# Causal attention on one core: the convolution's place on VectorE, an earlier norm of the memory, its filler matmuls spread over more steps, convolution sums in quarters, and four buffers moved

## The reference

```python
u = rmsnorm(h, norm_mix_pre)
bg, cg, xin, q, kc, vc, ksl, vsl, kw, vw, gl = split(u @ w_in)
z = cg * xin
y_conv = bg * conv3(z)                       # causal, 3 taps, one filter a channel, 512 channels
y_att = nsa_mixer(q, kc, vc, ksl, ...)       # three causal branches, 8 heads of 64
mixed = concat(rmsnorm(y_conv, norm_conv_out), rmsnorm(y_att, norm_attn_out))
h = h + rmsnorm(mixed @ w_out, norm_mix_post)
...
mn = rmsnorm(mem, norm_mem)                  # 256 memory tokens
kx, vx = split(mn @ w_kv_x)                  # for the cross attention behind
```

## Time and profile before

| | us |
|---|---|
| median of 3 runs (1782.98 to 1785.0) | 1784.61 |
| the profiled execution, its own time | 1782.14 |
| its span, first to last instruction | 1780.4 |
| PE busy in it | 1681.0 (94%) |
| mean granted TensorE clock | 0.979 |

### The profile page before, as it was taken

One profiled execution on the slowest core, in us unless ns is written; L12 is line 12 of the kernel. 1 busy time (PEld: TensorE's weight loads), 2 busy tenths in 40 slices (PEclk: granted clock), 3 DMA queues, 4 the chain that ended last, 5 costly groups with the idle time before them and its releaser, 6 DMA issues. The chain is left out here.

```text
span 1780.4 us, 22500 instructions
## 1 busy us (share of the span) xinstructions
PE 1681.0 (94%) x8603; PEld 1336.8 (75%) x8603; DVE 643.7 (36%) x1189; ACT 663.6 (37%) x1001; POOL 732.6 (41%) x639
## 2 busy tenths in 40 slices
PE   7989889988989999999989989998999999999999
PEld 5767668767668888878868767666678788888887
DVE  6431665262323111111147364443458341213131
ACT  4223377363344233222245434332554432323230
POOL 5223324363143444454435533332345444545453
PEclk9999899998999999999999999998999999999999
DMA  4243102232131332343222223221145323232321
GB/s 171 74 142 103 60 25 73 71 118 72 48 95 49 122 112 79 96 148 88 85 82 77 95 79 133 83 89 56 48 167 183 95 73 117 82 108 88 102 94 49
DMA packets 155307, 166.06 MB, mean 93 GB/s; under 512 B 14413, under 2 KB 116928, under 8 KB 155200
## 3 DMA queue, kind: packets, MB, share of 16 engines
q1 hardware_dynamic: 144736, 149.11, 26.2%
q10 hardware_dynamic: 10464, 15.51, 2.5%
HBM read 155.69 MB, written 9.30 MB: 93 GB/s over the span
## 5 line engine op out<-in xcount | busy, mean ns | idle before, releaser
L773 POOL TENSOR_TENSOR w_low<-raw,w_high 128x512 fp32r<-128x512 f32 x505 | 670.3, 1359 | 931.7 <-ACT w_high L916 931.3
L916 ACT CAST w_high<-raw 128x2048 fp32r<-128x2048 f32 (+1 forms) x128 | 241.1, 1884 | 251.5 <-PE bank L2306 240.4
L2311 PE MATMUL bank<-xT_high,w_high 128*128 128x512 f32 (+1 forms) x672 | 249.4, 376 | 0.0
L2312 PE MATMUL bank<-xT_low,w_high 128*128 128x512 f32 (+1 forms) x672 | 248.9, 375 | 0.0
L2302 PE MATMUL bank<-w_high,hid_high 128*128 128x512 f32 x432 | 171.9, 398 | 0.3 <-ACT w_high L916 0.3
L2303 PE MATMUL bank<-w_high,hid_low 128*128 128x512 f32 x432 | 169.8, 393 | 0.0
L2223 PE MATMUL bank<-xT_high,w_high 128*128 128x512 f32 (+1 forms) x360 | 154.3, 429 | 5.6 <-DVE xT_low L1527 3.2
L2315 PE MATMUL bank<-xT_high,w_low 128*128 128x512 f32 (+1 forms) x672 | 156.4, 375 | 0.6 <-POOL w_low L773 0.6
L2312 PEld LDWEIGHTS bank<-xT_low,w_high 128*128 128x128 f32 x672 | 127.5, 190 | 22.4
L2225 PE MATMUL bank<-xT_high,w_low 128*128 128x512 f32 (+1 forms) x360 | 144.3, 401 | 0.0
L2311 PEld LDWEIGHTS bank<-xT_high,w_high 128*128 128x128 f32 x672 | 127.4, 190 | 22.4
(11 more groups left out here) (425 smaller groups left out, 2567.2 us busy)
## 6 DMA issues: line engine op xcount, KB each, us to landing
raw<-in_w_in SPq DMA_DIRECT2D x33, 1024.0 KB, 5.0
raw<-in_w_down SPq DMA_DIRECT2D x26, 1024.0 KB, 5.0
raw<-in_w_gate_up SPq DMA_DIRECT2D x44, 512.0 KB, 5.0
raw<-in_w_up SPq DMA_DIRECT2D x16, 1024.0 KB, 5.3
raw<-in_w_kv_x SPq DMA_DIRECT2D x8, 1024.0 KB, 5.4
raw<-in_w_out SPq DMA_DIRECT2D x8, 1024.0 KB, 5.0
gate_dram<-qbuf ACTq DMA_DIRECT2D x20, 256.0 KB, 2.0
sg<-gate_dram ACTq DMA_DIRECT2D x6, 768.0 KB, 5.3
```

What stands on the lines that cost most here:

```text
L773: ins = pool.tensor_tensor(low[:, cs], full[:, cs], high[:, cs], ALU.subtract)
L916: own.tell(act.copy(split_slot(c, wh), split_slot(c, raw)), wh_done)
L2311: pe.matmul(ps[:, t0:t1], ch[:, k, cs], xh[:, k, t0:t1], start=q == 0, stop=False)
L2312: pe.matmul(ps[:, t0:t1], ch[:, k, cs], xl[:, k, t0:t1], start=False, stop=False)
```

## The change

- `conv` and `conv_scaled` run on DVE between the maximum of item s and the copy of item s-1, and no longer behind the copy and `branch_out`.
- The squares of the memory are summed on ACT in step 3 (`STAT_STEP`), DVE scales it in step 4 in place (`mem_nat` and not `stage`), PE transposes it in steps 9 and 10 (`MEM_STEP` 9).
- `kx` pieces begin at step 13: three a step, four in the last.
- The convolution's sums are made of 64 matmuls with 32 columns of weights each, one for each quarter of the partitions, in place of 16 with 128; they and the spread go to bank 3 and not bank 0, which makes PE wait for the second `o_taken` in step 10 and for the scaled tiles in step 14.
- `conv_root` calls a square root on a constant ahead of its wait, and an exponential behind the root.
- Buffers: the diagonal lies over `junk`, the convolution's output has its own place (`y_conv`), and the branch outputs lie in `share2`. That is also `gpost`, so its load waits for all eight `o_taken`, and is issued ahead of the first `vx` load and not ahead of `out`.
- ACT casts the second chunk of `out` ahead of the last square sum of the attention output.

```diff
@@ -39,6 +39,7 @@
...
 HALVES = (slice(0, 64), slice(64, P))
+QUARTERS = tuple(slice(32 * i, 32 * i + 32) for i in range(4))
 ATT_ORDER = (0, 3, 1, 2)
...
@@ -336,8 +337,8 @@
...
         yatt = at("yatt", 53312, [P, ST, S])
-        cdiag = at("conv_scale", 69696, [P, ST, P])
-        branch_early, branch_late = at("branch_early", 73792, [P, 2, S]), at("branch_late", 61504, [P, 2, S])
+        cdiag = nc.alloc_sbuf_tensor_at("conv_scale", [P, ST, P], F32, offset=junk_at)
+        yconv = at("y_conv", 69696, [P, 4, S])
         qn = at("qn", 53312, [P, 2, S])
...
@@ -517,8 +518,8 @@
...
         early, middle, late = pieces("bg"), pieces("cg", "xin"), pieces("kx")
-        CONV_STEP, SUM_STEP, MEM_STEP, KX_STEP = 5, 10, 14, 17
-        KX_N = [4] * 13 + [3] * 4
+        STAT_STEP, CONV_STEP, MEM_STEP, SUM_STEP, KX_STEP = 3, 5, 9, 10, 13
+        KX_N = [3] * 20 + [4]
         assert sum(KX_N) == len(late) and KX_STEP + len(KX_N) == 2 * ST * PER_GROUP + 2
...
@@ -534,7 +535,7 @@
...
-            return (branch_early if ph < 4 else branch_late)[:, ph % 2, :]
+            return share2[:, S * (ph % 2):S * (ph % 2) + S]
...
@@ -623,10 +624,10 @@
...
                 "kx": lambda: (late_mem(), bias_windows()),
-                "out": lambda: post_gain("norm_mix_post", None),
-                "ox": lambda: (post_gain("norm_x_post", ("h", 4)), natural_gain(0, "norm_ffn_pre", pv_done, 2 * ST * PER_GROUP)),
+                "vx": lambda: post_gain("norm_mix_post", o_taken, 2 * ST),
+                "ox": lambda: (post_gain("norm_x_post", h_ready, 4), natural_gain(0, "norm_ffn_pre", pv_done, 2 * ST * PER_GROUP)),
                 "down0": lambda: second_memory(),
-                "gu2": lambda: (post_gain("norm_ffn_post", ("h", 8)),
+                "gu2": lambda: (post_gain("norm_ffn_post", h_ready, 8),
                                 natural_gain(0, "g_mix_2", xn_ready, ntile["hf", 3] + 1)),
...
@@ -657,9 +658,8 @@
...
-            def post_gain(name, after):
-                if after:
-                    sp.wait_ge(h_ready, after[1])
+            def post_gain(name, dead, count):
+                sp.wait_ge(dead, count)
                 sp.dma_start(gpost[:, :], a[name].rearrange("(o d) -> o d", o=1).broadcast_to([P, D]))\
...
@@ -1021,13 +1021,15 @@
...
                 act.wait_ge(conv_y, ct + 1)
-                own.tell(act.activation(stage[:, ct // 2, (ct % 2) * S:(ct % 2) * S + S], bgT[:, ct, :], ACT.Square),
-                         conv_sq)
+                own.tell(act.activation(stage[:, ct // 2, (ct % 2) * S:(ct % 2) * S + S], yconv[:, ct, :],
+                                        ACT.Square), conv_sq)
...
             def conv_root():
+                own.link(act.activation(rms[:, 63:64], eps_col[:, 0:1], ACT.Sqrt))
                 act.wait_ge(conv_ss, 1)
-                own.tell(act.activation(small[:, 40:44], bank[0][:, 0:ST], ACT.Sqrt, bias=eps_col[:, 0:1],
+                own.tell(act.activation(small[:, 40:44], bank[3][:, 0:ST], ACT.Sqrt, bias=eps_col[:, 0:1],
                                         scale=1.0 / 512), conv_rms)
+                own.link(act.activation(rms[:, 63:64], eps_col[:, 0:1], ACT.Exp))
...
@@ -1071,11 +1073,12 @@
...
                     conv_square(s - CONV_STEP - 1)
-                if s == SUM_STEP:
-                    conv_root()
+                if s == STAT_STEP:
                     act.wait_ge(mem_in, 16)
...
                     stat(("mem", 1), mem_nat[:, 1, :], D)
+                if s == SUM_STEP:
+                    conv_root()
                 if SUM_STEP + 2 <= s < SUM_STEP + 4:
...
@@ -1086,6 +1089,7 @@
...
                                             scale=1.0 / 512), rms_done, 3)
+            high(G["out"].chunks[1].n)
             act.wait_ge(o_taken, 2 * ST)
...
@@ -1490,8 +1494,8 @@
...
                     return
-                own.tell(dve.tensor_scalar(stage[:, i % 2, 0:width], SOURCES[phase][:, j, :], rms[:, k:k + 1], None,
-                                           ALU.mult), xn_ready)
+                dst = mem_nat[:, j, :] if phase == "mem" else stage[:, i % 2, 0:width]
+                own.tell(dve.tensor_scalar(dst, SOURCES[phase][:, j, :], rms[:, k:k + 1], None, ALU.mult), xn_ready)
...
@@ -1666,7 +1670,7 @@
...
                 evacuated(dve, G["bg"].tiles[ct])
-                own.tell(dve.tensor_tensor(bgT[:, ct, :], qbuf[:, 0, :], bgT[:, ct, :], ALU.mult), conv_y)
+                own.tell(dve.tensor_tensor(yconv[:, ct, :], qbuf[:, 0, :], bgT[:, ct, :], ALU.mult), conv_y)
...
@@ -1682,8 +1686,8 @@
...
                     g = gcol[:, COL["norm_conv_out"] + ct:COL["norm_conv_out"] + ct + 1]
-                    own.tell(dve.scalar_tensor_tensor(out=qbuf[:, ct % 2, :], in0=bgT[:, ct, :], scalar=g,
-                                                      in1=bank[0][:, :], op0=ALU.mult, op1=ALU.mult), conv_q)
+                    own.tell(dve.scalar_tensor_tensor(out=qbuf[:, ct % 2, :], in0=yconv[:, ct, :], scalar=g,
+                                                      in1=bank[3][:, :], op0=ALU.mult, op1=ALU.mult), conv_q)
...
@@ -1739,6 +1743,10 @@
...
                             s_taken)
+                if CONV_STEP <= s < CONV_STEP + 4:
+                    conv(s - CONV_STEP)
+                if SUM_STEP + 2 <= s < SUM_STEP + 4:
+                    conv_scaled(2 * (s - SUM_STEP - 2))
                 if 1 <= s <= len(ITEMS):
...
@@ -1749,16 +1757,12 @@
...
                     own.tell(branch_out(branch_step(s)), o_taken)
-                if CONV_STEP <= s < CONV_STEP + 4:
-                    conv(s - CONV_STEP)
+                if s == STAT_STEP + 1:
+                    xn("mem", 0, D)
+                    xn("mem", 1, D)
                 if s == SUM_STEP + 1:
                     conv_inverse()
-                    xn("mem", 0, D)
-                    xn("mem", 1, D)
-                if SUM_STEP + 2 <= s < SUM_STEP + 4:
-                    conv_scaled(2 * (s - SUM_STEP - 2))
                 if MEM_STEP + 1 <= s < MEM_STEP + 3:
-                    dve.wait_ge(conv_lo, 4)
                     ql("mem", s - MEM_STEP - 1)
...
@@ -2206,15 +2210,16 @@
...
                     r = NT[i][3] + b
-                    if phase == "mem" and r == NT[ntile["mem", 0]][3]:
-                        pe.wait_ge(conv_q, 4)
+                    if phase == "mem" and j == 0:
+                        evacuated(pe, G["xin"].tiles[2 + b])
                     if r >= 2:
...
                             pe.wait_ge(q_ready, last[6] + r - 2 - last[3] + 1)
-                    src = hna[:, j, :] if phase == "hna" else hsum[:, j, :] if phase == "hm" else \
+                    src = mem_nat[:, j, 512 * b:512 * b + 512] if phase == "mem" else \
+                        hna[:, j, :] if phase == "hna" else hsum[:, j, :] if phase == "hm" else \
                         stage[:, i % 2, 512 * b:512 * b + 512]
...
@@ -2479,6 +2484,8 @@
...
                         pe.wait_ge(o_taken, ph - 1)
+                        if s == SUM_STEP + 4:
+                            pe.wait_ge(conv_q, 4)
                     for g in range(GROUPS):
...
@@ -2489,15 +2496,17 @@
...
                     pe.wait_ge(conv_sq, 4)
+                    pe.wait_ge(o_taken, 2)
                     for j in range(ST):
                         for ct in range(4):
-                            o = (ct % 2) * S + j * P
-                            mm = pe.matmul(bank[0][:, j:j + 1], stage[:, ct // 2, o:o + P], ones[:, 0:1],
-                                           start=ct == 0, stop=ct == 3)
+                            for qs in QUARTERS:
+                                o = (ct % 2) * S + j * P + qs.start
+                                mm = pe.matmul(bank[3][qs, j:j + 1], stage[:, ct // 2, o:o + 32], ones[:, 0:1],
+                                               start=ct == 0, stop=ct == 3)
                     mm.then_inc(conv_ss, 1)
...
                     pe.wait_ge(conv_inv, 1)
-                    pe.matmul(bank[0][:, :], ones[:, :], cdiag[:, :, :], start=True, stop=True).then_inc(conv_bc, 1)
+                    pe.matmul(bank[3][:, :], ones[:, :], cdiag[:, :, :], start=True, stop=True).then_inc(conv_bc, 1)
                 if MEM_STEP <= s < MEM_STEP + 2:
...
```

## The result

The changed kernel takes 1772.88 us (median of 4 runs, 1769.11 to 1773.33), the kernel before in the same comparison 1784.8 (1782.98 to 1785.46). The ratio is 0.9934, with a 95% interval of 0.9921 to 0.9947: about 0.7% faster. The prediction was 1774 us. The profiled execution took 1772.66 us, with a span of 1770.9, against 1782.14 and 1780.4.

A forecast was written before the change was run, and what follows sets the result against it. PE, busy 94% of the span, was taken as the bound, so gains come only where it idles or runs at low clock. Terms summed to -10.7 us, from the median 1784.61 to 1774 us; range 1766 to 1780.

The forecast's parts named there:

- Steps 6 and 7: Filler's waits for the convolution and the low clock behind them go, 6.71 us a step: -3.7 us.
- Steps 8 and 9: No filler; scores wait less for the maximum, the copy comes late next; 9.3 against 10.48 us: -1.2 us.
- steps 3 and 4: Memory's sums of squares on ACT (about 5.8 us) and scalings on DVE (2 us), hidden by filler: cost nil.
- Step 10: Low clock, sums by quarters at 5.7 us, memory transposes added; 13.8 against 9.67 us: +4.1 us.
- Quarters that don't overlap: Rival: each of 128 records costs its lone time, about 222 ns; sums 28 us, time 1797 us; 5 in 100.
- the clock stays up in steps 10 and 11: Rival: without the long waits PE keeps full clock there, some 5 us less; time 1768 us; 18 in 100.
- Step 11: Loses ACT's square sums and DVE's scalings, PE waits 0.3 us for the inverse; 7.0 against 6.59: +0.4 us.
- Steps 12 to 17: Waits and memory transposes go, 11 more filler pieces fit in; 23.8 against 27.52 us: -3.7 us.
- Steps 18 to 33: Twelve steps lose a filler piece, the last gains one, 0.36 us each: -4.0 us.
- `out`: Second chunk cast early; shorter wait, then for `xT_low`, and part of the low clock saved: -2.6 us.

The follow-up runs named there:

- c2: Changed kernel with ACT casting the first `kx` chunk in step 9 and not step 6, so POOL's split no longer meets the third convolution; 1768.98 us, ratio 0.9917.
- b4: Kernel before with only the convolution moved between maximum and copy on DVE; 1773.43 us, ratio 0.9943.
- c4: Kernel before with three edits only: convolution's place, sums by quarters, early cast of the second chunk of `out`; 1771.48 us, ratio 0.9935.
- a2: Changed kernel with the convolution's sums as 32 matmuls of 64 weight columns, alternating between two halves of the partitions; 1772.08 us.
- a3: Changed kernel with the same quarter matmuls, but all 16 of one quarter ahead of the next; 1773.75 us, ratio 0.9948.
- b2: Changed kernel with the old filler, `kx` pieces from step 17, four a step; 1774.06 us, ratio 0.9944.
- b3: Changed kernel without ACT's early cast of the second chunk of `out`; 1773.22 us, ratio 0.9942.
- c1: Changed kernel with ACT casting the memory's high part ahead of the root, and DVE inverting the scale ahead of step 11's maximum; 1770.47 us, ratio 0.9929.
- b1: Changed kernel with the convolution back behind the copy and `branch_out` on DVE; 1771.6 us, ratio 0.9931.
- c3: Changed kernel with both edits, the new order of steps 10 and 11 and the later cast of the first `kx` chunk; 1768.36 us, ratio 0.9909.
- a1: Changed kernel with the convolution's sums again as 16 matmuls of 128 weight columns, still in bank 3; 1772.15 us, ratio 0.994.

## Why the prediction was right, point by point

**Steps 6 and 7: right** in place and size. The two convolutions' waits are gone and each step takes 6.71 us.

**Steps 8 and 9: wrong**, +2.0 for -1.2. The step that failed is "In steps 5 to 7 that cover is some 5.5 us of pieces, enough to hide it." The 7.39 us beside POOL stood in the prediction, but wasn't set against the cover of step 7. That convolution begins 2.8 us into the step, behind the maxima, and at 7.1 us ends at 201.93, while PE is at the next step's transposes from 199.82. So PE waited 2.26 us, the low clock came at 203.78 and not 205, and the memory's transposes met it whole. c2 shows the cause: without POOL's split beside it, step 8 is as forecast. Step 9 stays at 7.45 us there, for 6.5: the low clock accounts for that 1.0.

A second step failed with it, in the passage on steps 3 and 4: DVE's two scalings of the memory delay a maximum "which is wanted a step later. Cost nil". First a scaling in the kernel after, then the start of the third convolution and PE's wait in b4, which has no scalings in step 4:

```profile
178.93 0.75 DVE L1498 TENSOR_SCALAR mem_nat<-mem_nat,rms 128x1024 f32<-128x1024 f32 x1
```

```profile
194.74 0.69 DVE L1662 TENSOR_TENSOR zT<-zT,bank 128x512 f32<-128x512 f32 x1
201.90 0.30 PE L2200 MATMUL bank<-ident,prob 128*128 128x128 f32 x1 [1.02 <-DVE probT L1750]
```

From the scalings on DVE has next to no idle time in the kernel after until step 10. Its third convolution begins 2.80 us into step 7 and takes 7.08, in b4 1.97 into the step and takes 6.68. So PE waits 2.26 us and not 1.02, and step 8 takes 5.02 and not 3.79 (3.79 in c4 too, which leaves the memory where it was). The memory's place was not taken back by itself, so the 1.2 us are read from kernels that differ in more. b4 isn't the forecast come true either: its steps 8 and 9 take 9.40 us, but without the memory's 1.7 the prediction would have had 7.6.

**Step 10: wrong**, -2.0 for +4.1, the largest error. The step that failed is "I take the middle, 5.7 us (45 ns each)". Measured are 1.16 us, 9 ns each, below the lower bound of 3.9, which supposed that a quarter of the columns costs a quarter of the time, one matmul behind the other. The bound is for the low clock, but half of it, 1.9 us as an estimate for the full one, is still more than was measured. It left out that four quarters can work at once. The rival "Quarters that don't overlap" at 222 ns a record falls too, but the forecast's own 45 ns were also a price for one matmul behind the other. The floor of 60 cycles in the Trainium skill (TensorEngine Tiling (Array Packing), Instruction Overhead), 6.4 us here, doesn't hold for matmuls that take turns over the quarters: at full clock 60 cycles are 25 ns, and 9 were measured. It fits a2 and a3 better, with 31 and 33 ns. The same page of the Trainium skill (TensorEngine Tiling (Array Packing), Key Properties) also says that different tiles can load weights and multiply in parallel. a3 against the kernel after shows it, 33 ns against 9. The other 3.0 us are the clock, which was full again from 213.00, ahead of the sums and not behind them; a wait of 1.58 us for the second `o_taken`, where 0.2 were counted, took 1.4 back. 5.7 - 1.16 + 3.0 - 1.4 = 6.1, the whole miss. In part the rival "the clock stays up in steps 10 and 11" came true, though the clock didn't stay up: it fell earlier and rose earlier.

**Step 11: right by two errors.** PE ran at full clock, and so was early: "PE is then still at the memory's transposes and the scores of item 11 (3.9 us), so nothing is lost" failed, as these took 2.1 us. DVE waited 2.59 us for ACT, and PE 3.07 and not 0.3 for the inverse. In b2 and b3 part of the step ran at low clock and the wait was 1.44 and 1.49, and the step took 7.37 and 7.34 us all the same: the chain of ACT and DVE set its length and not PE's clock. c1 takes the wait away by order alone. The table loads were read rightly. ACT's timeline of the kernel after:

```profile
218.12 0.26 ACT L1030 ACTIVATE small<-bank,eps_col 128x4 f32<-128x4 f32 x1 [0.24 <-PE bank L2504]
218.40 1.28 ACT L1032 ACT_TABLE_LOAD   x1
219.69 0.20 ACT L1032 ACTIVATE rms<-eps_col 128x1 f32<-128x1 f32 x1
```

Nothing of the drain for which the Trainium skill (ScalarE: Activation LUTs, What ACT_TABLE_LOAD costs) adds 1.38 us is seen on either side of the load.

**Steps 3 and 4: right for these steps.** ACT's work on the memory runs from 172.49 to 178.07 in the shade of the filler; steps 3 to 5 take 6.7 us each. That DVE's scalings come due in step 8 is told above.

**Steps 12 to 17: right but for the clock**, -2.7 for -3.7. Step 12 began behind the 3.07 us wait, its scores lasted 2.08 us and the step 4.77, where 3.35 was counted. Steps 13 to 17 took 20.08, 20.4 were counted. Where that wait was 1.44 to 1.66 us (a2, b1, b2, b3, c2) or absent (c1) step 12 took 3.36 to 3.64.

**Steps 18 to 33: right**, -3.9 for -4.0. PE's timeline shows 2.94 us a step, and step 18 at 251.16 for "near 252":

```profile
251.16 0.70 PE L2466 MATMUL bank<-kT,qT 64*128 64x256 f32 x4
254.10 0.70 PE L2466 MATMUL bank<-kT,qT 64*128 64x256 f32 x4
```

**`out`: right**, -2.2 for -2.6. The one wait left is the one named, for `xT_low`, at the size forecast:

```profile
317.63 0.50 PE L2307 MATMUL bank<-w_high,xT_high 128*128 128x512 f32 x1 [2.35 <-DVE xT_low L1531]
```

The missing 0.4 are the low clock behind it, counted at 0.7 us of a possible 1.8; in this run it stayed, 1.6 us.

**The whole.** The miss of step 10, -6.1, is met by +3.2 in steps 8 and 9 and by +0.4, +1.0, +0.1 and +0.4 in the four behind step 10: together -1.0, so that -10.7 came out as -11.6 (rounding aside). So the time is nearer to the forecast than its reasons deserve. The span fell by 9.5 only: step 0 began 0.3 us later, and behind the copy the kernel after took 1.8 us more. 1.2 of these are PE's wait for `w_low` at L2320, 1.8 us after and 0.6 before at the same line; c3 has the 1.8 too. Why it is longer was not tried.

What the prediction didn't see is that the parts stand in for one another. They were added as if each came on top. But each of the four edits that were taken back one by one (a1, b1, b2, b3) left the time where it was, while the convolution's place alone, or three edits (c4), bring about as much as all. The memory's move was not taken back by itself; c4 does without it. The stretch from step 8 to 12 has no filler; PE's pace there is set by the queues of DVE and ACT, and by a clock that falls behind some waits and not behind others. In step 11 what makes PE sooner makes it wait longer, until the late instruction itself is moved, as in c1. For the rest of the stretch this is argued and not shown, and why b4 alone gains 10.2 us of time stays open in part. Why the clock falls behind one 2.35 us wait in `out` and not behind the same wait in another run stays open.

## What to carry to other kernels

Where one engine's instruction is hidden behind another's work, compare the latest end with the cover, and take for its duration that beside the engines which run then: here 7.1 us and not 3.55. Don't add the gains of single edits in a stretch where PE idles; find what is late next, and move that instruction in its queue, which here gave 3.4 to 5.1 us of the trace for the same work. And set two profiled executions of the same instructions side by side before putting a difference of 2 us down to an edit. Small matmuls with few weight columns should take turns over the quarters of the columns.

## What of the hardware was not expected

- 128 matmuls with 32 columns of weights and one of data take 1.16 us when consecutive ones go to different quarters (9 ns each, granted clock 1.00), and 4.26 us when they stay in one (33 ns, 0.87). Whole ones, 128 columns wide, take 138 ns each at a granted clock of 0.80.
- DVE's instructions with two operands in SBUF take about twice as long beside POOL's subtractions, 3.34 us for 1.54 and 1.63 for 0.69, and one with a single operand there 1.31 for 0.49; the one that reads a bank takes 0.69 both times. The Trainium skill (SBUF — State Buffer, SBUF: two separate sides) has the two engines take their shared ports in turn for a whole instruction; the traces agree in that each such instruction grew by 0.8 to 0.9 us, less than one of POOL's (1.4).
- The same instructions in steps 5 to 12 took 50.45 to 52.46 us, by where the clock was low. The same 2.35 us wait brought a clock of 0.64 over the next 14 matmuls in one run and 1.00 in another.
